# A two-layer decoder trunk on one core: the beginning, the ends of the token mixers and the routing to the experts are rearranged

## The reference, cut to what matters

```python
for l in range(2):
    x = x + token_mixer(rms_norm(x, attn_norm[l]), ...)   # q, k, v, low-rank q and kv, two attentions,
                                                          # two branch projections, sigmoid gates, @ w_out
    h = rms_norm(x, ffn_norm[l])
    if l == 0: x = x + swiglu(h, w_gate_up, w_down)       # width 2816
    else:                                                 # top 2 of 8 experts of the same width
        logits = h @ router_w
        top_v, top_i = top_k(logits, 2); probs = softmax(top_v)
        x = x + sum over e of gate[:, e] * swiglu(h, w_gu[e], w_down[e])
```

## Time and profile before

| | us |
|---|---|
| three runs | 1386.8, 1389.71, 1392.05; median 1389.71 |
| profiled execution, its own time | 1389.64 |
| its span | 1387.8 |
| mean granted clock of TensorE | 0.991 |
| PE busy in the span | 1341.6 |
| DVE busy | 1050.8 |
| ACT busy | 885.4 |

### The profile page before, as it was taken

How to read it: one execution, slowest core, us unless ns; L and a number is a source line. 1 busy time by engine, 2 the same in 40 slices (tenths; PEclk the granted TensorE clock), 3 DMA queues, 4 the chain that set the end, 5 groups by cost and what they waited for, 6 DMA issues and landing times.

```text
span 1387.8 us, 19264 instructions
## 1 busy us (share of the span) xinstructions
PE 1341.6 (97%) x7170; PEld 1174.5 (85%) x7170; DVE 1050.8 (76%) x975; ACT 885.4 (64%) x916; POOL 81.5 (6%) x67
## 2 busy tenths in 40 slices
PE   6999989999999999889999999999999999999996
PEld 6889978888988899877888888988888889889886
DVE  4786666544457875668889898898898898988984
ACT  6575546443456754446777687776776776877773
POOL 0320000000002200000000000000000010000000
PEclk9999999999999999989999999999999999999999
DMA  7633345655546424497999999999999999999991
GB/s 241 226 97 122 123 152 192 204 190 164 175 155 216 122 92 147 142 392 286 322 377 380 374 386 380 373 381 389 371 382 373 382 380 373 378 389 371 382 354 53
DMA packets 180669, 381.29 MB, mean 275 GB/s; under 512 B 8666, under 2 KB 63620, under 8 KB 180612
## 3 DMA queue, kind: packets, MB, share of 16 engines
q1 hardware_dynamic: 177520, 369.94, 74.5%
q0 software_dynamic: 2304, 8.39, 2.3%
q10 hardware_dynamic: 788, 2.18, 0.4%
HBM read 374.20 MB, written 6.29 MB: 274 GB/s over the span
## 4 chain that ended last, share of the span: by engine, by line
PE 85%; DVE 6%; ACT 4%; issue 3%; DMA 1%; ACTq 0%; DVEq 0%; POOLq 0%
PE ps L1048 17%; PE ps L1050 17%; PE ps L1049 17%; PE ps L648 7%; PE ps L650 7%; PE ps L649 7%; PE ps L655 2%; PE ps L657 2%; PE ps L656 2%; PE ps L1101 1%; ACT w_hi L1206 1%; DVE w_lo L1538 1%; DVE mix L1730 1%; DVE w_lo L1791 1%; PE ps L773 1%
## 5 line engine op out<-in xcount | busy, mean ns | idle before, releaser
L1791 DVE TENSOR_TENSOR w_lo<-mix,w_hi 128x2048 fp32r<-128x2048 f32 (+2 forms) x192 | 394.8, 2068 | 81.5 <-ACT w_hi L1411 80.5
L1411 ACT CAST w_hi<-mix 128x2048 fp32r<-128x2048 f32 (+2 forms) x190 | 329.4, 1738 | 129.4 <-PE ps L1050 129.4
L1048 PE MATMUL ps<-w_hi,eT_hi 128*128 128x512 f32 (+1 forms) x768 | 289.8, 377 | 1.1 <-DVE eT_lo L1933 1.1
L1538 DVE TENSOR_TENSOR w_lo<-raw,w_hi 128x2048 fp32r<-128x2048 f32 (+4 forms) x94 | 198.7, 2120 | 116.1 <-ACT w_hi L1206 114.9
L1049 PE MATMUL ps<-w_lo,eT_hi 128*128 128x512 f32 (+1 forms) x768 | 285.8, 372 | 0.0
L1050 PE MATMUL ps<-w_hi,eT_lo 128*128 128x512 f32 (+1 forms) x768 | 285.6, 372 | 0.0
L1206 ACT CAST w_hi<-raw 128x2048 fp32r<-128x2048 f32 (+4 forms) x94 | 166.4, 1777 | 140.3 <-PE ps L650 98.7
L1791 DVE TENSOR_TENSOR w_lo<-raw,w_hi 128x2048 fp32r<-128x2048 f32 (+1 forms) x96 | 209.6, 2200 | 17.4 <-ACT w_hi L1411 16.8
L1411 ACT CAST w_hi<-raw 128x2048 fp32r<-128x2048 f32 (+1 forms) x96 | 175.3, 1843 | 40.6 <-PE ps L1050 37.7
L1048 PEld LDWEIGHTS ps<-w_hi,eT_hi 128*128 128x128 f32 x768 | 144.7, 188 | 20.4 <-DVE eT_lo L1933 1.2
L1050 PEld LDWEIGHTS ps<-w_hi,eT_lo 128*128 128x128 f32 x768 | 144.5, 188 | 20.4
(11 more groups left out here) (200 smaller groups left out, 1943.9 us busy)
## 6 DMA issues: line engine op xcount, KB each, us to landing
mix<-in_expert_w_gate_up_dram SPq DMA_DIRECT2D x79, 1024.0 KB, 7.7
raw<-in_expert_w_gate_up_dram SPq DMA_DIRECT2D x49, 1024.0 KB, 7.7
mix<-in_expert_w_down_dram SPq DMA_DIRECT2D x49, 1024.0 KB, 8.3
mix<-in_expert_w_gate_up_dram SPq DMA_DIRECT2D x48, 768.0 KB, 8.5
raw<-in_expert_w_down_dram SPq DMA_DIRECT2D x31, 1024.0 KB, 8.7
raw<-in_w_in_dram SPq DMA_DIRECT2D x28, 1024.0 KB, 5.5
raw<-in_dense_w_gate_up_dram SPq DMA_DIRECT2D x16, 1024.0 KB, 5.2
raw<-in_expert_w_gate_up_dram SPq DMA_DIRECT2D x16, 768.0 KB, 8.6
```

Of the source, the lines that this page charges most:

```text
L1048: pe.matmul(out_, l_hi, w_hi[q][:, cols], start=first, stop=False, skip_group_check=True)
L1411: act.copy(w_hi[q][:, 0:m], e_raw[raw_of(p, first)][:, 0:m]).then_inc(e_hi_ready, 1)
L1538: dve.tensor_tensor(w_lo[q][:, 0:m], raw[u % RAW][:, 0:m], w_hi[q][:, 0:m].bitcast(F32), ALU.subtract).then_inc(split, 1)
L1791: dve.tensor_tensor(w_lo[q][:, 0:m], e_raw[raw_][:, 0:m], w_hi[q][:, 0:m].bitcast(F32), ALU.subtract).then_inc(e_split, 1)
```

## The change

Nothing of what is computed for the output changes. The order of the work, one place in which a factor is applied, and the form of the first gather do.

- Beginning: the mixers' norm gains (16 rows, `gcol_first`) are loaded first and alone, ahead of the identity; the others follow and are turned later, into another bank. An ACT operation without use (`Square` of a constant) stands ahead of ACT's first wait. PE makes 12 bf16 products of 128x512 on a constant before its first wait for data and 12 after `turn_normed(0, 0)`.
- Mixer ends: DVE's splits of the last units stand after merges 0, 3, 4 and (two) 5 in place of 0, 2, 4, 5 and the end; ACT's rounding of the last unit stands ahead of merge 6. In the second mixer t=1 of the projection is finished half by half of the columns, for its last two units.
- Routing: ranking works on unscaled logits, and the scaling follows it. PE makes 12 products of 128x256 ahead of its wait for `chosen_b` and 14 after counting. The one-hot matrix (`first_hot`, times the norm factor) is the stationary matrix and x the moving one, in four products of 512 columns; DVE multiplies by the gain row into `first_h`, and PE turns that in eight transposes. Softmax, item count and `one_hot(1, 1)` are moved behind the gather and one split. `keep_rows(1)` and the copy of x to `out` move into item 0 on ACT, behind unit 8; `gained(1)` and `places_next(1)` move into item 0 on DVE.
- Item 0: its first products wait for half of the gathered tokens; `turn_e(0, 0)` stands in the middle of the second block, not ahead of it.

```diff
+        warm = mix[:, o_qka:o_qka + T].bitcast(BF16)
...
+        first_hot = mix[:, o:o + NT * CAP].rearrange("p (t c) -> p t c", t=NT)
+        first_h = mix[:, 0:D]
...
+                for w in range(4):
+                    project_out(0, w, range(2))
+                for w in range(2):
+                    project_out(1, w, range(2))
+                if l == 0:
+                    turn_normed(1, 0)
+                    for w in range(2, 4):
+                        project_out(1, w, range(2))
+                else:
+                    turn_x(0, range(2))
+                    for half in range(2):
+                        for w in range(2, 4):
+                            project_out(1, w, (half,))
...
+                def logits(t, half):
+                    evacuated(tile["xT", t, half])
+                    for kt in range(4 * half, 4 * half + 4):
                         last = pe.matmul(ps[r_.bank][:, t * NEXP:(t + 1) * NEXP], xT[:, kt, t * P:(t + 1) * P],
                                          router[:, kt, :], start=kt == 0, stop=kt == DT - 1)
-                last.then_inc(filled[r_.bank], 1)
+                    return last
+
+                pe.wait_ge(router_set, 1)
+                start(r_)
+                turn_x(1, (0,))
+                logits(0, 0)
+                turn_x(1, (1,))
+                logits(0, 1)
+                logits(1, 0)
+                logits(1, 1).then_inc(filled[r_.bank], 1)
...
+                both = cst[:, CONST["earlier"][0]:CONST["ones"][1]].bitcast(BF16)
+                for _ in range(12):
+                    pe.matmul(ps[1][:, 0:2 * P], before, both, start=True, stop=True)
...
                 last.then_inc(filled[n_.bank], 1)
+                for _ in range(14):
+                    pe.matmul(ps[1][:, 0:2 * P], before, both, start=True, stop=True)
...
-                if not (first and j == 0):
+                if first and j == 1:
+                    pe.wait_ge(e_silu, 1)
+                elif not (first and j == 0):
                     pe.wait_ge(hid_done, i * FF + j)
                 for piece in range(4):
                     p = up_at(j) + piece
+                    if first and j == 1 and piece == 2:
+                        turn_e(i, 0, first)
+                    if first and j == 0 and piece < 2:
+                        pe.wait_ge(gath_lo, piece + 1)
...
                 pe.wait_ge(first_sel, 1)
-                pe.wait_ge(h_gained, NT)
+                for half in range(2):
+                    for t in range(NT):
+                        last = pe.matmul(ps[4 + half][:, :], first_hot[:, t, :], x[:, t, half * 512:(half + 1) * 512], start=t == 0,
+                                         stop=t == NT - 1)
+                    last.then_inc(first_rows, 1)
                 for g in range(2):
+                    pe.wait_ge(first_staged, g + 1)
                     for m in range(4):
-                        cols = slice((4 * g + m) * P, (4 * g + m + 1) * P)
-                        for t in range(NT):
-                            last = pe.matmul(ps[6 + g][:, m * CAP:(m + 1) * CAP], h[:, t, cols], sel[:, t, :], start=t == 0,
-                                             stop=t == NT - 1)
+                        last = pe.transpose(ps[6 + g][:, m * CAP:(m + 1) * CAP], first_h[:, (4 * g + m) * P:(4 * g + m + 1) * P],
+                                            ident)
                     last.then_inc(gath_done, 1)
...
             def item(i, first=False):
-                pe.wait_ge(gath_lo, i * 2 + 2)
+                if not first:
+                    pe.wait_ge(gath_lo, i * 2 + 2)
                 gate_up_e(i, 0, first)
+                if first:
+                    places(1)
+                else:
+                    down_last(i)
                 if not first:
-                    down_last(i)
-                turn_e(i, 0, first)
+                    turn_e(i, 0, first)
...
+            pe.wait_ge(warm_set, 1)
+            for _ in range(12):
+                pe.matmul(ps[6][:, :], warm[:, 0:P], warm, start=True, stop=True)
             pe.wait_ge(ident_in, 16)
+            pe.wait_ge(first_gain_in, 16)
+            pe.transpose(ps[7][:, 0:FIRST_GAINS], gcol_first, ident[0:FIRST_GAINS, 0:FIRST_GAINS]).then_inc(gcol_turned, 1)
+            turn_normed(0, 0)
+            for _ in range(12):
+                pe.matmul(ps[6][:, :], warm[:, 0:P], warm, start=True, stop=True)
             pe.wait_ge(gain_in, 16 * GAIN_ROW_DMAS)
-            pe.transpose(ps[7][:, 0:2 * GL], gcol_rows, ident[0:2 * GL, 0:2 * GL]).then_inc(gcol_turned, 1)
-            turn_normed(0, 0)
+            n = 2 * GL - FIRST_GAINS
+            pe.transpose(ps[6][:, FIRST_GAINS:2 * GL], gcol_rest, ident[0:n, 0:n]).then_inc(gcol_turned, 1)
...
+            act.dma_start(gcol_first, a["attn_norm"].rearrange("l (r c) -> (l r) c", c=P)).then_inc(first_gain_in, 16)
             act.dma_start(cst[:, 0:P], a["consts"][:, 0:P]).then_inc(ident_in, 16)
-            for name, w, n in (("attn", "attn_norm", DT), ("ffn", "ffn_norm", DT), ("cq", "mla_cq_norm", 3),
-                               ("ckv", "mla_ckv_norm", 2)):
-                r = DEPTH * G0[name]
-                act.dma_start(gcol_rows[r:r + DEPTH * n, :], a[w].rearrange("l (r c) -> (l r) c", c=P)).then_inc(gain_in, 16)
+            for name, w, n in (("ffn", "ffn_norm", DT), ("cq", "mla_cq_norm", 3), ("ckv", "mla_ckv_norm", 2)):
+                r = DEPTH * G0[name] - FIRST_GAINS
+                act.dma_start(gcol_rest[r:r + DEPTH * n, :], a[w].rearrange("l (r c) -> (l r) c", c=P)).then_inc(gain_in, 16)
+            act.wait_ge(half_set, 1)
+            act.activation(ss_h[:, 0, :], half_neg[:, :], ACT.Square)
...
-                    if m in (1, 3, 4):
-                        hi(u0 + {1: 25, 3: 26, 4: 27}[m])
+                    if m in (1, 3, 4, 6):
+                        hi(u0 + {1: 25, 3: 26, 4: 27, 6: 28}[m])
                     act.wait_ge(merged_sum, DT * l + m + 1)
                     act.copy(merged[0][:, m, :], prod[:, m % 2, 0:T]).then_inc(merged_hi_set, 1)
-                hi(u0 + 28)
...
+            def keep_rows(t):
+                act.wait_ge(h_gained, t + 1)
+                act.dma_start(h_rows[t * P:(t + 1) * P, :], h[:, t, :]).then_inc(h_out, 16)
+
             square(3, 0)
             copy_high_e(0, 0, True)
+            turned_x(0)
             copy_high_e(0, 1, True)
-            turned_x(0)
+            keep_rows(0)
...
+                    if p == 8 and first:
+                        keep_rows(1)
+                        act.dma_start(out[0].rearrange("(t p) c -> p t c", p=P), x[:, :, :]).then_inc(x_out, 16)
...
-                    if m in (0, 2, 4, 5):
-                        lo(u0 + {0: 24, 2: 25, 4: 26, 5: 27}[m])
+                    for n in {0: (24,), 3: (25,), 4: (26,), 5: (27, 28)}.get(m, ()):
+                        lo(u0 + n)
                 merged_low(DT - 1)
-                lo(u0 + 28)
...
             add_to_x(0, "wo", 1)
-            split_low_e(0, 0, True)
-            split_low_e(0, 1, True)
-            turned_x(0)
             dve.wait_ge(g_row_in, 16)
             gained(0)
-            add_to_x(1, "wo", 1)
+            split_low_e(0, 0, True)
+            turned_x(0)
+            add_to_x(1, "wo", 1, halves=(0,))
+            split_low_e(0, 1, True)
+            add_to_x(1, "wo", 1, halves=(1,))
             turned_x(1)
-            gained(1)
...
+            step(dve.tensor_copy(lg, raw_lg))
...
-            dve.tensor_scalar(chosen, tmp16, TOPK - 0.5, None, ALU.is_lt)
+            step(dve.tensor_scalar(chosen, tmp16, TOPK - 0.5, None, ALU.is_lt))
+            dve.wait_ge(norm_rstd, 8)
+            dve.tensor_tensor(lg, raw_lg, rs_x.unsqueeze(2).broadcast_to([P, NT, NEXP]), ALU.mult).then_inc(drained[t_.bank], 1)
+            dve.wait_ge(drained[t_.bank], t_.done)
             step(dve.reduce_max(r2[0], lg, AX_X))
             dve.tensor_tensor(less, lg, r2[0].unsqueeze(2).broadcast_to([P, NT, NEXP]), ALU.subtract).then_inc(route_ready, 1)
-            dve.wait_ge(sel_bits, 1)
-            dve.wait_ge(route_exp, 1)
+            dve.wait_ge(route_ready, 1)
...
-                last = dve.tensor_scalar(sel[:, t, :], con("slot_no"), route[:, t, 1:2], None, ALU.is_equal)
+                last = dve.tensor_scalar(first_hot[:, t, :], con("slot_no"), route[:, t, 1:2], rs_x[:, t:t + 1], ALU.is_equal, ALU.mult)
             last.then_inc(first_sel, 1)
...
+            for half in range(2):
+                cols = slice(half * 512, (half + 1) * 512)
+                dve.wait_ge(first_rows, half + 1)
+                dve.tensor_tensor(first_h[:, cols], ps[4 + half][:, :], g_row[:, cols], ALU.mult).then_inc(first_staged, 1)
...
                         hidden_e(i, 0, unit_no(i, 3) + 1)
+                        if first:
+                            gained(1)
+                            places_next(1)
...
             gathered(0)
-            places_next(1)
```

(12 more changed lines are left out.)

116 lines of the change are left out of this document (47 added, 69 removed).

## The result

| | before | after |
|---|---|---|
| median of the runs, us | 1388.81 (1386.80 to 1392.05, 4 runs) | 1371.16 (1370.79 to 1372.09, 4 runs) |
| profiled execution, span | 1387.8 | 1369.0 |
| its granted clock, mean | 0.991 | 0.997 |

The ratio of the times is 0.9872, 95% interval 0.9851 to 0.9892: faster by 1.3%. The prediction was 1368.0 us, 1362 to 1377. Step by step it was right in the mixer ends, nearly right in the routing and in item 0, and 1.8 us too hopeful at the beginning.

The account below looks back on a forecast made before the run. TensorE, 85% of the chain that ended last, sets the time by its work, waits and slow clock. Beginning -5.0, mixer ends -10.6, routing -4.1 and item 0 -1.8 sum to -21.5: 1368.1 us, range 1362 to 1377.

Parts of the forecast that it names:

- Beginning, -5.0: Start: gains and identity land at 5.9 us, first product at 11.0, 4.2 earlier, some 0.8 more kept; -5.0 us.
- Mixer ends, -10.6: Ends of both mixers: TensorE's waits for merge 3 and the last split go, with the slow clock; -5.3 us each.
- Routing, -4.1: From the end of t=0 to the first expert product: 26.0 us instead of 30.1, -4.1.
- (a): Routing, from the end of t=0 to the logits: 16.4 us instead of 18.5.
- (c): Routing, one-hot columns to first expert product: 5.4 us instead of 6.65, with the gather at full clock.
- (b): Routing, logits to one-hot columns: 4.2 us instead of 5.0, with the filling products fitting into TensorE's waits.
- Item 0, -1.8: First expert product to `down`: 24.6 us instead of 26.4, including a 1.7 us wait for unit 9.
- Rival 1: Clock not held at the start and in the gather, item 0 without gain: -16.0 us, 1374; chance 15%.
- Rival 2: Mixer ends: the last split's load lands 3 us later than forecast, -2.3 us each, 1374; chance 12%.
- Rival 3: Experts bound by their loads, so what routing and item 0 gain is lost: -15.6 us, 1374; chance 5%.
- Rival 4: Item 1's fetched rows come late because x to `out` is issued later; TensorE waits 29.5 us, 1398; chance 2%.
- rival 6: More gained than summed, with unit 9 in time and all of the start kept: 1364 us; chance 5%.

Follow-up runs that it names:

- Experiment 5: Changed kernel with the identity issued ahead of the first gains and the constants behind the fourth weight unit: 1369.61 us.
- experiment 7: Changed kernel without the early activation, so that ACT loads its table in front of the first real one: 1371.70 us.
- experiment 2: Changed kernel with the splits at both mixer ends back in their old places: 1382.16 us.
- experiment 3: Changed kernel with only one mixer-end edit left, unit 25 split behind merge 3; unit 28 rounded and split last as before: 1376.74 us.
- experiment 10: The changed kernel itself measured once more, on the same chip as experiment 9: 1371.71 us.
- 8: Kernel of experiment 3 with fourteen filling products in TensorE's wait for the last split, in both mixers: 1375.06 us.
- experiment 9: Changed kernel with the edits of Experiment 5 and experiment 6 together, but ten filling products ahead of the gather: 1368.12 us.
- experiment 6: Changed kernel with five filling products instead of fourteen ahead of the gather, and the rows of t=1 stored behind unit 10 instead of 8: 1369.45 us.
- experiment 1: Changed kernel without its 50 filling products, nothing else: 1374.29 us.
- 4: Kernel before with the change's edits of the beginning and the mixer ends, routing and item 0 as before: 1377.22 us.

## Why the prediction was right, and where it was not

Point by point, with the terms as they stand on record.

- **Beginning, -5.0: measured -3.2.** The step that was too hopeful is "I take 5.9 us for both" and, behind it, "later loads wait for splits and move along". The identity took 5.6 us from its issue instead of 4.7, and the first product came at 11.86 instead of 11.0. The fourth unit's load did move along, but took 5.2 us to land where it took 4.1 in the kernel before, and TensorE waited 0.73 us. The likely cause is that the constants' 449 KB stand ahead of it in the queue and had not landed yet (issued at 3.4, landed after 9.5 us; the unit is issued at 11.7, in the kernel before at 15.1). Experiment 5 gives back 1.4 of the 1.8 by moving these transfers alone, with the first product at 10.99. The size of the table load was right to 0.01 us (experiment 7).
- **Mixer ends, -10.6: measured -11.1** (4.9 and 6.2, of which 0.5 is not the end's by experiment 2). Both waits, their separateness and the chain of five merges and four splits came out as worked: the last low part was to be written at 194.7, less the start's 3.2, and was at 191.5. The thin cover held. Undone, the term comes back as 11 us (experiment 2), and of it 1.8 us a mixer, without the clock, is the last split (experiment 3).
- **Routing, -4.1: measured -3.6** in the profiled execution and -2.3 in another of the same kernel (experiment 10). (a) 16.3 us for 16.4; (c) 5.4 for 5.4. The step that was mis-sized is (b), 4.8 for 4.2: "fourteen, 1.5 us (3.0), into the rest" fits at the full clock only, and they took 2.80. I had both paces in the text and took the better one for the sum. Where the clock stays up, in the profiles of 5, 8 and 9, they do fit, and (b) is 4.3.
- **Item 0, -1.8: measured -2.1.** ACT rounds unit 9 at +17.1 (forecast 17.5), and the wait is 1.04 instead of 1.7. The forecast's own terms, 22.7 and 1.7, make 24.4 and not the 24.6 of the sum, so 0.2 of the difference is a slip of mine. That the store's place is the cause was argued there; experiment 6 shows it.
- **Not in the sum: +1.2 us in the rest**, 1.1 of it behind the rows that are turned last, in item 7, where TensorE is idle at two places with nothing that the profile names to wait for.

```profile
1355.20 0.49 PE L1073 MATMUL ps<-w_hi,e_hidT_hi 128*128 128x512 f32 x1 [2.35 <-issue]
...
1358.40 0.50 PE L1074 MATMUL ps<-w_lo,e_hidT_hi 128*128 128x512 f32 x1 [0.64 <-issue]
```

The first of them is not new: the kernel before stands there as well, for the low part of the last hidden block, and only 0.3 us of the 1.1 were added to it. The second is the other 0.8.

```profile
1374.91 0.49 PE L1048 MATMUL ps<-w_hi,e_hidT_hi 128*128 128x512 f32 x1 [2.09 <-DVE e_hidT_lo L1945]
```

With 1.8 at the beginning, 0.5 in the routing, 1.2 in the rest, less 0.5 in the mixer ends and 0.3 in item 0, the profiled execution is 2.7 us above the 1368.1. The total was met as closely as it was in part because errors of both signs stood in it.

The rivals. Rival 1, the clock not held where it matters, fell (experiment 1), though not in the way I thought: in the profile of after the filling products did not keep the clock up in the router, they took the slow stretch on themselves. Rival 2, the last split late, did not come. Rival 3 fell: from the first rows that are turned in item 0 to the last that are turned in item 7 it is 659.7 us in the kernel before,

```profile
L1116 PE MATMUL ps<-cst,h_scaled x64: 272/272/273, 700.0 to 1359.7; 128*128 128x128 f32 x64
```

and in the changed one,

```profile
L1147 PE MATMUL ps<-cst,h_scaled x64: 272/272/273, 680.1 to 1339.8; 128*128 128x128 f32 x64
```

so all 19.9 us gained by then are kept over the length of seven items, at a DMA share of 1.03. Rival 4 with its late rows did not come either; no wait stands ahead of item 1. Of rival 5, an unseen wait, the run has a small one, the 0.8 us among the last eighteen products; rival 6, all of the start kept and unit 9 in time, came only after the repairs of experiment 9.

## What to carry to other kernels

An engine that prepares work for the one that sets the time does it in some order, and the order alone was worth 11 us here. What paid was to do first what frees a bank for which the other engine waits, and last what the fewest of its products need. Filling products are worth the slow stretch that they take on, less what they delay when they run at half pace themselves: count them for the lower clock. And when a start is made earlier, the loads ahead of it don't follow by themselves; look at what stands in front of each in its queue, and at what of that nobody wants yet.

## What the runs showed of the hardware that was not expected

- The new routing takes 26.4 us in six profiles (2, 3, 5, 6, 8, 9), 26.7 in that of after and 28.0 in 7 and 10, and TensorE's instructions are the same in after, 2, 3, 5, 7 and 10. It hangs on where in the router's small products the clock falls to 0.50, or whether it does. It fell in all three profiles without the filling products (before, 1, 4) and in six of the nine with them; in 5, 8 and 9 it stood at 1.00 throughout the routing. That the filling products ahead of the counting have a part in that is not shown. Where it fell late (2, 3), or under five filling products (6), the gather still began within 0.2 us of the earliest, and the routing took the same 26.4 us.
- The same wait is followed by a slow stretch in one execution and not in another: 1.90 us with the clock at 1.00 behind it in the first mixer of the kernel before (7.3 us from there to the first `w_out` product; the window is below), at 0.50 in experiment 2 (8.8 us). One execution shows it both ways: in the profile of before the clock falls behind the second wait (2.14 us) of the first mixer and not behind the first, and in the second mixer behind the first (1.91 us; 0.57 over 568 to 572) and not behind the second (1.00 over 586 to 592). The wait of 2.05 to 2.55 us ahead of the last eighteen products is another such case: behind it the clock fell in 1 and 9 and in none of the ten others.
- TensorE pauses in the last eighteen products with no wait that the profile shows, behind the tenth, for 0.3 to 0.8 us beyond the pace of 0.23: in all six profiles of kernels whose TensorE instructions are those of the changed one, and in none of the six others (before, 1, 4, 6, 8, 9). It goes with the instruction's place in the code; what it is stays open, and no kernel tried to move it.
- The granted clock says little about a start: the window from 1 to 6 us shows 1.00 while the first ten of the twelve products of 512 columns keep a pace of 0.43 us.

The window behind the first wait of 1.90 us in the kernel before (busy times of PE, PEld, DVE, ACT, POOL; granted clock, DMA share, GB/s):

```profile
179.00:183.00 4.00, 2.73 (x22) 2.73 (x23) 1.98 (x4) 1.67 (x3) 0.00 (x0) 1.00 0.58 174
```
